# Overflow half-blocks moved between the seventh and eighth expert, and the last two expert pairs combined by a gate matrix

## The reference, cut to what matters

```python
def _moe(h, router_w, router_bias, w_gate, w_up, w_down):
    ...
    wsel = jnp.take_along_axis(scores, idx, axis=-1)
    wsel = wsel / jnp.sum(wsel, axis=-1, keepdims=True)
    gates = jnp.sum(jax.nn.one_hot(idx, N_EXPERTS, dtype=jnp.float32) * wsel[..., None], axis=1)
    a = jnp.einsum('td,edf->tef', x, w_gate)
    up = jnp.einsum('td,edf->tef', x, w_up)
    mid = jax.nn.silu(a) * up * gates[:, :, None].astype(x.dtype)
    y = jnp.einsum('tef,efd->td', mid, w_down)
    ...
def layer(x, l, mod, mixer):
    ...
    x = x + g2 * _moe(h, router_w, router_bias, moe_w_gate[l], moe_w_up[l], moe_w_down[l])
```

## Time and profile before

| | us |
|---|---|
| median of 3 runs | 961.86 (958.14 to 964.68) |
| the profiled execution | 958.43 |
| its span | 956.6 |
| TensorE busy in it | 798.8 |
| granted clock of TensorE, mean | 0.914 of full |
| moved by DMA | 232.21 MB, mean 243 GB/s |

### The profile page before, as it was taken

One profiled execution on the slowest core, in us unless ns is written; L12 is line 12 of the kernel. 1 busy time (PEld: TensorE's weight loads), 2 busy tenths in 40 slices (PEclk: granted clock), 3 DMA queues, 4 the chain that ended last, 5 costly groups with the idle time before them and its releaser, 6 DMA issues.

```text
span 956.6 us, 11465 instructions
## 1 busy us (share of the span) xinstructions
PE 798.8 (84%) x4035; PEld 440.2 (46%) x4035; DVE 378.3 (40%) x844; ACT 271.0 (28%) x631; POOL 95.1 (10%) x146
## 2 busy tenths in 40 slices
PE   4879999999879987999771779878899989998750
PEld 0237665635434555555330445545554565554320
DVE  3376673354253341421113434664643334221114
ACT  1242112210541231222112325555532322221111
POOL 3200000001000013000004002211200030000002
PEclk8589999999989996999995779999999969999995
DMA  9991174369960287999997936202115589999965
GB/s 287 368 330 46 44 175 140 119 232 322 310 247 0 69 315 247 401 411 411 411 374 244 375 100 256 90 1 90 46 46 219 196 321 399 413 410 412 389 246 197
DMA packets 85055, 232.21 MB, mean 243 GB/s; under 512 B 7188, under 2 KB 17101, under 8 KB 84681
## 3 DMA queue, kind: packets, MB, share of 16 engines
q1 hardware_dynamic: 72706, 193.89, 55.6%
q0 software_dynamic: 8576, 27.38, 8.6%
q10 hardware_dynamic: 3720, 10.25, 2.9%
HBM read 216.60 MB, written 17.78 MB: 245 GB/s over the span
## 4 chain that ended last, share of the span: by engine, by line
PE 58%; DMA 17%; DVE 8%; issue 7%; SPq 4%; ACT 3%; DVEq 2%; POOLq 1%; POOL 0%; ACTq 0%
PE ps L868 52%; DMA ring<-in_moe_w_up_dram 7%; PE ps L875 4%; DMA arena<-in_moe_w_up_dram 3%; SPq L654 2%; DMA ring<-in_w_mod_dram 2%; PE ps L1095 2%; DVEq L1842 1%; SPq L637 1%; DVE negmax L1895 1%; DMA h_rows<-xn 1%; DMA arena<-y_rows,rows_out 1%; DMA hT<-h_rows,rows_in 1%; DVE xn L2286 1%; ACT hT L1557 1%
## 5 line engine op out<-in xcount | busy, mean ns | idle before, releaser
L868 PE MATMUL ps<-arena 128*64 128x256 f32 (+13 forms) x1084 | 229.4, 453 | 30.1 <-DMA arena<-in_moe_w_down_dram 7.5
L868 PEld LDWEIGHTS ps<-arena 128*64 128x64 f32 (+4 forms) x1084 | 123.5, 171 | 119.6 <-issue 67.0
L868 PE MATMUL ps<-ring,hT 128*128 128x512 f32 (+2 forms) x384 | 134.5, 509 | 6.5 <-issue 5.9
L868 PE MATMUL ps<-ring,arena 128*64 128x256 f32 (+1 forms) x864 | 126.1, 435 | 15.0 <-DMA ring<-in_moe_w_up_dram 7.3
L868 PEld LDWEIGHTS ps<-ring,hT 128*128 128x128 f32 x384 | 73.2, 193 | 64.2 <-issue 59.8
L868 PEld LDWEIGHTS ps<-ring,arena 128*64 128x64 f32 x864 | 60.9, 137 | 65.0 <-issue 39.3
L875 PE MATMUL ps<-ident,arena 128*128 128x128 f32 (+2 forms) x332 | 50.6, 292 | 21.1 <-DVE hT L1901 5.6
L1514 ACT ACTIVATE arena<-ps 128x256 f32<-128x256 f32 (+5 forms) x88 | 38.7, 454 | 94.1 <-PE ps L868 87.5
L2226 DVE TENSOR_TENSOR arena<-arena,ps 128x128 f32<-128x128 f32 x37 | 10.7, 288 | 133.3 <-ACT arena L1619 133.3
L868 PE MATMUL ps<-hT,ring 128*128 128x384 f32 x192 | 62.1, 486 | 0.0
L868 PE MATMUL ps<-ring,condT 128*32 128x512 f32 x384 | 53.1, 682 | 7.6 <-DMA ring<-in_w_mod_dram 6.9
(11 more groups left out here) (295 smaller groups left out, 833.6 us busy)
## 6 DMA issues: line engine op xcount, KB each, us to landing
ring<-in_w_mod_dram SPq DMA_DIRECT2D x48, 1024.0 KB, 8.8
ring<-in_moe_w_down_dram SPq DMA_DIRECT2D x24, 1024.0 KB, 17.8
ring<-in_moe_w_gate_dram SPq DMA_DIRECT2D x42, 512.0 KB, 14.0
ring<-in_moe_w_up_dram SPq DMA_DIRECT2D x42, 512.0 KB, 16.3
arena<-in_moe_w_gate_dram SPq DMA_DIRECT2D x32, 512.0 KB, 8.5
arena<-in_moe_w_up_dram SPq DMA_DIRECT2D x32, 512.0 KB, 10.2
arena<-in_moe_w_down_dram SPq DMA_DIRECT2D x13, 1024.0 KB, 13.3
ring<-in_ev_w_in_dram SPq DMA_DIRECT2D x9, 1024.0 KB, 13.1
```

What stands on the lines that cost most here:

```text
L868: mm = pe.matmul(out, lhsT, rhs, **kw)
```

## The change

The overflow half-blocks run between expert 6 and expert 7 (`OVER_AT = 7`) on all engines, with semaphores of their own. For that, the lists of overflow rows are made earlier (TensorE's part behind expert 3's down product, VectorE's at place 5), expert 6's down product stands ahead of the loop, and SyncE sends the blocks' weights ahead of the third round of refills, behind one refill of slot 2. At its end SyncE waits until the last block is through.

Pairs 6 and 7 (experts 12 to 15) are no longer stored: `y_rows` keeps zeroes there (the zero fill of the start is larger by 256 rows). The six gathers wait for the stores up to pair 5's, and bring zeroes for rows of the last four experts. `scale_first` and `join` of all three tiles stand at place 14 of the loop. For the last two pairs VectorE makes a matrix for each pair that holds, for a token and a slot, the gate or zero (`plan_spread`, places 9 and 10); TensorE turns it (`spread_turn`, place 13), and multiplies it with the results in SBUF (`tail_product`). VectorE multiplies by `gb`, and GpSimd adds to `x`. In layer 0 `mixer_turn(1, 1)` now stands ahead of `latent_in(0)`. SyncE's wait ahead of the second layer's attention weights is for the early slots and not for the gathers.

```diff
@@ -45,7 +45,9 @@
 NMAIN = NE * HALF
 NROWS = NMAIN + NOVER * HALF
 NEARLY, CYCLES = 5, 3
-EXPERT_ORDER = [(e, kind) for n in range(NE + 1) for e, kind in ((n, 0), (n, 1), (n - 1, 2)) if 0 <= e < NE]
+OVER_AT = 7
+EXPERT_ORDER = [(e, kind) for n in range(NE + 1) for e, kind in
+                (((n, 0), (n, 1), (n - 1, 2)) if n != OVER_AT else ((n - 1, 2), (n, 0), (n, 1))) if 0 <= e < NE]
 
 
...
@@ -53,6 +55,9 @@
     for _slot in range(NEARLY):
         EARLY[EXPERT_ORDER[_cycle * (NEARLY + RING) + _slot]] = (_slot, _cycle)
 OVER_SLOT = (0, 1, 4)
+OVER_IX = OVER_AT % 2
+NSTORED = NPAIR - 2
+TAIL_BANKS = (0, 1, 2, 4, 6, 3)
...
+                    if cycle == CYCLES - 1:
+                        at[f"over{l}"] = len(pieces)
...
-                        if kh == 0:
-                            sp.wait_ge(over_free[l], b + 1)
-                        else:
-                            sp.wait_ge(gu_full[l], b + NE)
+                        sp.wait_ge((over_free, over_gu_full)[kh][l], b + 1)
...
+                for freed in (over_free, over_gu_full, over_done):
+                    sp.wait_ge(freed[l], nb + 1)
...
-                if i == at["after0"]:
-                    send_over(0)
                 if i == at["in1.1"] + 1:
-                    for t in range(NT):
-                        sp.wait_ge(y_back[t], 32)
+                    sp.wait_ge(early_used, NEARLY * CYCLES)
...
-                for slot, used, again in refill.get(i, ()):
+                entries = refill.get(i, ())
+                for l in range(2):
+                    if i == at[f"over{l}"]:
+                        entries = [entry for entry in entries if entry[0] not in OVER_SLOT]
+                        for slot, used, again in entries[:1]:
+                            sp.wait_ge(early_used, used)
+                            fill_early(slot, again)
+                        send_over(l)
+                        entries = [entry for entry in refill[i] if entry[0] in OVER_SLOT] + entries[1:]
+                for slot, used, again in entries:
                     sp.wait_ge(early_used, used)
                     fill_early(slot, again)
                 send(i, entry)
-            send_over(1)
...
-            pool.dma_start(y_rows[NMAIN:NROWS, :], d["zero_row"].partition_broadcast(NROWS - NMAIN)).then_inc(rows_zeroed, 16)
+            pool.dma_start(y_rows[P * NSTORED:NROWS, :], d["zero_row"].partition_broadcast(NROWS - P * NSTORED)).then_inc(rows_zeroed, 16)
...
-                    pool.wait_ge(y_stored[c][l], 16 * (NPAIR // 2))
+                    pool.wait_ge(y_stored[c], 16 * (NSTORED // 2) * (l + 1))
...
+                for t in range(NT):
+                    for half in range(2):
+                        drained_wait(pool, f"tail{l}", 2 * t + half)
+                        cols = slice(512 * half, 512 * half + 512)
+                        pool.tensor_tensor(x[:, t, cols], x[:, t, cols], xn[:, t, cols], ALU.add)
+                    pool.drain().then_inc(x_done, 1)
...
+                    nb = blocks_of(pe, l)
+                    with pe.Fori(0, nb) as b:
+                        pe.wait_ge(over_xt_read[l], b * 2 + 2)
+                        for kh in range(2):
+                            pe.wait_ge(over_full[kh][l], b * 32 + 32)
+                            mm = gate_up(kh, ps[GU_BANKS[OVER_IX]], xgT[:, 0, :, 0:HALF], four(early_w[:, OVER_SLOT[kh], :]))
+                            mm.then_inc((over_free, over_gu_full)[kh][l], 1)
+                        pe.wait_ge(over_gathered[l], b * 16 + 32)
+                        turn_in(xg_over, (None, over_xt_full[l]))
+                        turn_mid(OVER_IX, over_mid[l], b + 1, over_mt_full[l])
+                        pe.wait_ge(over_mt_read[l], b + 1)
+                        pe.wait_ge(over_done[l], b + 1)
+                        pe.wait_ge(over_y_read[l], b + 1)
+                        pe.wait_ge(over_full[2][l], b * 16 + 16)
+                        mm = down(OVER_IX, early_w[:, OVER_SLOT[2], :].rearrange("p (j n) -> p j n", n=D))
+                        mm.then_inc(over_y_full[l], 1)
+                    pe.wait_ge(over_xt_read[l], nb * 2 + 2)
+                    main_turn(OVER_AT // 2 + 1)
+                    pe.wait_ge(over_done[l], nb + 1)
+                    pe.wait_ge(over_y_read[l], nb + 1)
...
+                def spread_turn():
+                    pe.wait_ge(spread_ready, l + 1)
+                    for half in range(2):
...
+                def tail_product(i, c):
+                    t, half = divmod(i, 2)
+                    bank = claim(f"tail{l}", i) if c == 0 else ps[TAIL_BANKS[i]]
+                    mm = product(bank[:, :], slot_to_row[:, c, t, :], ysb[:, c, 512 * half:512 * half + 512], carries=c == 0, start=c == 0, stop=c == 1)
+                    if c:
+                        fill_inc(mm, f"tail{l}", i)
...
-                    if e:
+                    if e and e != OVER_AT:
                         main_mid(e - 1)
                     main_gate_up(e, 1)
-                    if e % 2 == 0:
+                    if e == OVER_AT - 1:
+                        over_turn()
+                    elif e % 2 == 0 and e // 2 + 1 < NPAIR:
                         main_turn(e // 2 + 1)
-                    if e:
+                    if e == NE - 1:
...
+                            drained_wait(pe, f"spread{l}", c)
+                        for half in range(2):
+                            pe.wait_ge(y_read[half], NE * l + NE - 2)
+                        tail_product(0, 0)
+                        tail_product(1, 0)
+                    if e and e != OVER_AT:
                         main_down(e - 1)
-                    if e == 6:
-                        bank = ps[MT_BANKS[0]]
-                        pe.wait_ge(over_hit[l], 1)
-                        for i in range(2 * NT):
-                            mm = product(bank[0:HALF, 256:256 + NOVER], hit_over[:, i, :], place_block[:, 16 * i:16 * i + NOVER], start=i == 0, stop=i == 2 * NT - 1)
-                        mm.then_inc(over_idx[l], 1)
+                    if e == 4:
+                        over_rows_list()
+                    if e == OVER_AT - 1:
+                        main_mid(e)
+                        main_down(e)
+                        overflow()
+                    if e == NE - 3:
+                        spread_turn()
...
+                tail_product(2, 0)
+                tail_product(3, 0)
                 main_down(NE - 1)
-                turn(ps[MT_BANKS[0]][:, 0:P], ident[:, :])
-                pe.wait_ge(y_read[0][l], NE - 1)
-                nb = blocks_of(pe, l)
-                with pe.Fori(0, nb) as b:
...
-                    for kh in range(2):
-                        pe.wait_ge(over_full[kh][l], b * 32 + 32)
-                        mm = gate_up(kh, ps[GU_BANKS[0]], xgT[:, 0, :, 0:HALF], four(early_w[:, OVER_SLOT[kh], :]))
-                        mm.then_inc(gu_full[l] if kh else over_free[l], 1)
...
+                for half in range(2):
+                    pe.wait_ge(y_read[half], NE * l + NE - 1)
+                tail_product(4, 0)
+                tail_product(5, 0)
+                for half in range(2):
+                    pe.wait_ge(y_read[half], NE * l + NE)
+                for i in range(2 * NT):
+                    tail_product(i, 1)
...
+                    with act.Fori(0, nb) as b:
+                        act.wait_ge(over_gu_full[l], b + 2)
...
+                        result(ysb[0:HALF, 0, 0:512], OVER_IX, over_done[l])
+                        act.wait_ge(over_done[l], b + 2)
+                        act.wait_ge(over_y_read[l], b + 2)
+                        act.dma_start(y_rows[bass.ds(b * HALF + NMAIN, HALF), :], ysb[0:HALF, 0, :]).then_inc(over_stored[l], 16)
...
+                    if e == NE - 2:
+                        scale_first(l, 0)
+                    if e and e != OVER_AT:
                         main_turned(e - 1)
...
+                    if e == NE - 2:
+                        scale_first(l, 1)
+                    if e == OVER_AT - 1:
+                        act.wait_ge(over_xt_full[l], 1)
+                        rows_copy(xgT[:, 0, 0:4, 0:HALF], HALF, over_xt_read[l])
+                    elif e % 2 == 0 and e // 2 + 1 < NPAIR:
+                        pair_rows(e // 2 + 1)
...
+                    if e % 2 == 0 and 0 < e <= 2 * NSTORED:
+                        store(e // 2 - 1)
+                    if e == NE - 2:
+                        scale_first(l, 2)
+                    if e == OVER_AT - 1:
+                        main_turned(e)
+                        main_result(e)
+                        nb = overflow()
+                        pair_rows(OVER_AT // 2 + 1)
+                    if e == NE - 3:
+                        copy_out(f"spread{l}", 0, slot_to_row[:, 0, :, :].rearrange("p a b -> p (a b)"), bank_of(f"spread{l}", 0)[:, 0:NT * P])
                 main_turned(NE - 1)
                 main_result(NE - 1)
```

(45 more changed lines are left out.)

354 lines of the change are left out of this document (178 added, 176 removed).

## The result

Four runs of the changed kernel gave 979.90 us (978.06 to 982.87), four of the kernel before 962.45 us. The ratio is 1.019, with a 95% interval of 1.0144 to 1.0235: the change makes the kernel 1.9% slower. The forecast was 964 (950 to 977). The profiled execution took 978.76 us, its span is 976.8 us.

A forecast was written before the change was run, and what follows sets the result against it. Expert stages were bound by DMA of weights, with an exposed end behind them. Layer 0 gained 0.6 us, layer 1 ended at 959.0 against 956.6: +2.4, so 960.8, or 964 on the median's scale; range 950 to 977.

The forecast's parts named there:

- rival (c): Behind the experts: y gathers wait as long as weights, 19.5 us, 12 us later per layer, 988; 0.06 with Rival (d).
- R: Moment TensorE gets past the overflow loop and starts expert 7; forecast 450.5 us in layer 0, 874.2 in layer 1.
- T: End of down(15), the last expert's down product; forecast 522.4 us in layer 0, 946.1 in layer 1.
- S: Start of expert 0's first product in a layer; 371.0 to 376.1 us in layer 0 of the profiled executions.
- step 1: Stage end: loop, store, gather, joins leave; block weights save no DMA; y gathers cost 7.6 us, fewer stores return 2.5.
- steps 2 and 3: Overflow loop, layer 0: TensorE waits some 6 us for weights; down products at 436.6 and 447.2; DMA loss 444 to 454.
- Rival (b): Overflow loop gets weights later: block 0's down piece lands at 440.5, not 436; +12.8 us in all, 977; chance 0.19.
- Step 4: From R to the eleventh expert's result: 36.2 us, with the weights keeping up.
- step 5: Pair 5's store, y gathers and joins at place 14 give T = R + 71.9; about 6.6 us lost per layer.
- Rival (a): Stage end bound by weights alone, joins fit in waits: T = R + 65.3, -13.2 us, 951; chance 0.25 with mixtures.
- step 6: Tail behind the last down product: layer 0's projection ends at T + 31.4, layer 1 ends at T + 12.9.
- Rival (d): Tail doesn't get shorter than its 28 us: layer 1 alone 15 us longer than summed, 979; 0.06 with rival (c).

The follow-up runs named there:

- loop-alone kernels: Changed kernel without gate matrix and tail products, all eight pairs stored, joins behind the experts: 982.2 us; with free-place pieces sent early and attention weights held: 964.4 us.
- the tail merged: Against the kernel with joins behind the last products: tile 2's join takes matrix products in before the multiply, layer 0's norm steps reordered; 956.6 us, 0.9939 of before.

## Why the prediction was wrong

The chain that bound the stage was the forecast one; one link of it was mis-sized in the way of rival (c), which had been dismissed. The sum was 18.0 us short of the profiled execution (960.8 against 978.76). Its own terms, on the trace's clock:

| term | predicted | measured | off by |
|---|---|---|---|
| R, layer 0 | 450.5 | 450.9 | 0.4 |
| R to T, layer 0 | 71.9 | 76.2 | 4.3 |
| T to the projection's end | 31.4 | 34.4 | 3.0 |
| projection's end to S of layer 1 | 231.9 | 233.6 | 1.7 |
| S to R, layer 1 | 88.5 | 92.4 | 3.9 |
| R to T, layer 1 | 71.9 | 74.2 | 2.3 |
| T to the end | 12.9 | 15.0 | 2.1 |

(88.5 is 874.2 less 785.7, the old 786.28 with the 0.6 us gained in layer 0. The seven add up to 17.7.) All are on the same side, so misses of 0.4 to 4.3 us made 2%. The two of R to T are the largest share, 6.6 us; the two of the tail are 5.1, and layer 1's S to R is 3.9.

**What leaves the end (step 1)** was half right. It said that the y gathers' bytes would share the DMA with weights, and charged 7.6 us of DMA time; what mattered was the gathers' own landing.

**When the loop gets its weights, and the loop (steps 2 and 3)** held in layer 0 to 1 us: the end of the wait ahead of the loop (430.4 for 430, though partly by luck: expert 6 was done 2 us later and the wait 2 us shorter than summed), the cadence (10.8 us, 10.6 forecast), and the hole, with R at 450.9. (The recorded 0.6 us for a product at the lower clock is 0.85 by its own rows; here that product ran at the full clock.) The hole was forecast from 444 to 454; from 447 to 451 only 7 GB/s moved. The loop-alone kernels measure its price: 7.8 and 10.8 us lost, and 6.3 per layer between R and T back with three pieces in it. Rival (b) fails: the first down product of the loop waited 0.61 us for ScalarE in both layers, and not for its weights. In layer 1 the blocks stand 12.2 and 10.8 us apart (11.1 summed), and the last product and turn ran at a granted clock of 0.60 (2.99 and 1.67 us for 1.94 and 1.09); that makes 2.4 us more than the sum. The other 1.5 of layer 1's 3.9 us are in layer 0 too (R - S was 79.1 for 77.6) and hidden there by an S that came 1.1 us earlier.

**Step 4** held: pair 5's store was issued at R + 35.9 in both layers (37.2 summed).

**The new chain (step 5) is the step that failed.** "The second one 7.5 us to land", taken from a row_now gather, was the mis-sized term, and with it the spacing of the joins. GpSimd's first gather left at R + 44.5 (44.2 summed). But tile 0's rows could be scaled only 10.0 us later, in layer 1 10.7 (8.75 summed), and the tiles behind it came 5.3 and 7.0 us apart, in layer 1 5.3 and 5.2, where I had the three joins follow each other at VectorE's 4.06 us. So the third join started at R + 68.0, in layer 1 at R + 66.0, instead of R + 63.4; from there to T it is 8.2 us in both (8.5 summed), so this step's whole miss lies in the gathers. This is rival (c) in part, which I had put at 19.5 us for a gather, deciding from 11.7, and dismissed: the last gather took 16.0 and 15.0 us from issue to use. Its sign, y gathers of more than 11 us, was there. They shared the DMA with the weights half and half rather than waiting behind them. Between 7.5 and 19.5 I took the lower end, by a single gather that had no others ahead of it. Six in a row are 10 us for the first pair and, at half of the DMA's rate, 1.05 MB / 0.2 = 5.2 us for each further pair (why layer 0's last pair took 7.0 stays open). Step 1 had their bytes in its sum, but step 5 gave them no time beyond the first pair.

**Place 14 as the binding chain** was right. It was to cost 6.6 us per layer over the weights' floor (R + 65.3); with the joins one place later T - R fell by 7.3 and 6.0 us, to 68.9 and 68.2, and TensorE waited for weights. (The floor itself was summed 3.6 and 2.9 us too low.) Rival (a) therefore fails: in the changed kernel TensorE waited for weights for only 1.2 us in layer 0's last 42 us before T, so the gathers and joins had no such waits to fit into.

**The tail (step 6)** was mis-sized by 3.0 and 2.1 us. GpSimd's pair of additions took 2.50 us where 1.9 was estimated, 1.8 us in three pairs, the whole of layer 1's miss but 0.3. In layer 0 the projection started 14.6 us after T (13.5 forecast), and its first third ran at a granted clock of 0.71 (7.84 us instead of 5.7). Rival (d) fails: the end is 15.0 us behind the last down product instead of 28.

**Costed at nothing:** plan_spread, plan_gates and the turns hid as said (TensorE runs from R to expert 12 without a wait). The early attention weights cost the changed kernel nothing (T - R off by 0.6 with them held); in the loop-alone kernel, where the gathers would have had the DMA to themselves, they cost 8.5 us. The 1.7 us between the layers stay open: the stretch was 231 to 236 us in all kernels.

Why a large change moved the time so little, and the wrong way: the moved loop by itself loses 7.8 and 10.8 us, of which filling the idle DMA gives 6.3 back in each layer; what the gate matrix then takes off the end is spent on joins and gathers that stand ahead of TensorE's last experts. With the hole filled, the joins behind the last products and the tail merged, the same ideas give 956.6.

## What to carry to other kernels

Work moved from an exposed end into a stage bound by DMA was only free here once the DMA went on through it: look for what the engine that issues the DMAs waits for at the end of the moved work, and send ahead of that wait what already has a free place. What is put ahead of the last products to be hidden must not wait for a transfer that shares the DMA with those products' weights; place it behind them, and it fills the wait instead of making one. For a chain of gathers, cost the bytes of all of them at a shared rate, not the latency of one.

## What the runs showed of the hardware

Gathers of GpSimd's queue beside a full SyncE queue moved 200 of 410 GB/s; alone 400 to 410 (1.59 MB in 8 us and 1.64 MB in 4 us, shown above).

VectorE and GpSimd slowed each other where both read two operands in SBUF: in the kernel with the joins one place later, GpSimd's second pair of additions took 4.07 us instead of 2.50 and VectorE's two steps beside it 2.13 instead of 1.23 each. VectorE's multiplies that read PSUM stayed at 0.69 beside the same additions. It is not only a matter of two operands: in the changed kernel the norm's step of 1024 float32, which reads one tensor in SBUF, took 1.29 us (535.64) and 1.52 us (538.33) beside GpSimd's additions, and 0.80 us (541.88) behind them.

```profile
957.42 4.07 POOL L840 TENSOR_TENSOR x<-x,xn 128x512 f32<-128x512 f32 x2 [0.69 <-issue]
...
958.24 2.13 DVE L2432 TENSOR_TENSOR xn<-xn,gb 128x1024 f32<-128x1024 f32 x1
```

The Trainium skill ("SBUF — State Buffer", "SBUF: two separate sides") has them share a port pair as an exclusive lock, which one holds for a whole instruction while the other waits. The rows agree in kind: 2.13 is 1.23 and most of one addition (1.25).
